# Moving two groups of VectorE work from between a scan and its use to behind the step, in the S5 loop of a two-block kernel

## The reference

```python
z = rms_norm(h, pre_mix_norm) @ w_in
z_rw, z_nsa, z_s5 = split(z)
o_rw  = rwkv7_mixer(token_shift(z_rw), ...)
o_nsa = nsa_mixer(z_nsa, ...)     # per query: compressed keys, selected keys, window keys
o_s5  = s5_mixer(z_s5, ...)       # y = C * linear_scan(lambda, B u), then a gated output
mix = concat([o_rw, o_nsa, o_s5]) @ w_out

# compressed branch of nsa_mixer, 15 compressed positions, 6 query heads
k_cmp = gelu(blocks(kc) @ w1_k) @ w2_k
v_cmp = gelu(blocks(vc) @ w1_v) @ w2_v
p_c = masked_softmax(q @ k_cmp.T * scale - slopes * distance)
o_c = p_c @ v_cmp
```

## Time and profile before

| what | value |
|---|---|
| median of 3 runs | 1343.27 us |
| the 3 runs | 1342.36, 1343.27, 1344.06 us |
| the profiled execution's own time | 1342.36 us |
| its span, first to last instruction | 1340.4 us |
| TensorE busy with matmuls | 1278.5 us (95%) |
| VectorE busy | 564.4 us (42%) |
| ScalarE busy | 621.8 us (46%) |
| GpSimd busy | 849.0 us (63%) |
| mean granted TensorE clock | 0.974 of full speed |

### The profile page before, as it was taken

The page is one execution under the profiler, slowest core; times in us unless marked ns, Lnnn a source line. Parts: engine busy times, 40 slices in busy tenths (PEclk is TensorE's granted clock), DMA queues, the critical chain, the costliest instruction groups (busy, mean ns, idle before and its releaser), DMA issues.

```text
span 1340.4 us, 25785 instructions
## 1 busy us (share of the span) xinstructions
PE 1278.5 (95%) x10737; PEld 1192.8 (89%) x10737; DVE 564.4 (42%) x1275; ACT 621.8 (46%) x962; POOL 849.0 (63%) x441
## 2 busy tenths in 40 slices
PE   7998989889999999899999999999999998999998
PEld 6984548679999999899999999999998888999998
DVE  5658686633666653513333203132222224433301
ACT  5531443136655644653544434554534454544442
POOL 7985400027798696564887786856745665788772
PEclk9998999989999999898999999999999999999999
DMA  8749995504455555334555554453648793455550
GB/s 266 205 158 371 345 334 206 189 1 158 145 177 183 173 174 188 126 122 162 165 182 189 173 174 157 145 165 98 191 127 263 233 291 123 139 181 188 174 173 32
DMA packets 232817, 242.82 MB, mean 181 GB/s; under 512 B 9068, under 2 KB 201726, under 8 KB 232702
## 3 DMA queue, kind: packets, MB, share of 16 engines
q1 hardware_dynamic: 232382, 241.08, 55.3%
q10 hardware_dynamic: 320, 0.10, 0.0%
HBM read 240.11 MB, written 1.05 MB: 180 GB/s over the span
## 4 chain that ended last, share of the span: by engine, by line
PE 83%; DVE 4%; ACT 2%; issue 1%; DVEq 0%; ACTq 0%
PE banks L548 81%; PE banks L1332 1%; DVE arena L1693 1%; DVE arena L1686 1%; ACT arena L2432 1%; DVE banks L1686 0%; DVE banks L1693 0%; ACT ring_hi L2432 0%; DVE arena L1699 0%; ACT hn_hi L2432 0%; PE banks L558 0%; PE banks L861 0%; PE banks L984 0%; ACT L2432 0%; DVE arena L1690 0%
## 5 line engine op out<-in xcount | busy, mean ns | idle before, releaser
L1613 POOL TENSOR_TENSOR ring_lo<-ring,ring_hi 128x2048 fp32r<-128x2048 f32 (+1 forms) x176 | 719.0, 4096 | 423.5 <-ACT ring_hi L2432 423.4
L548 PE MATMUL banks<-hn_hi,ring_lo 128*128 128x256 f32 (+1 forms) x1864 | 525.4, 287 | 0.0
L548 PE MATMUL banks<-hn_hi,ring_hi 128*128 128x256 f32 x1696 | 484.0, 289 | 11.8 <-ACT hn_hi L2432 11.0
L548 PE MATMUL banks<-hn_lo,ring_hi 128*128 128x256 f32 x1696 | 445.8, 283 | 0.0
L2432 ACT ACTIVATE ring_hi<-ring 128x2048 fp32r<-128x2048 f32 (+1 forms) x176 | 299.6, 1704 | 171.2 <-PE banks L548 127.3
L548 PEld LDWEIGHTS banks<-hn_hi,ring_lo 128*128 128x128 f32 (+1 forms) x1864 | 363.6, 196 | 0.1
L548 PEld LDWEIGHTS banks<-hn_hi,ring_hi 128*128 128x128 f32 x1696 | 333.1, 196 | 15.2 <-issue 9.4
L548 PEld LDWEIGHTS banks<-hn_lo,ring_hi 128*128 128x128 f32 x1696 | 310.5, 192 | 0.1
L2432 ACT ACTIVATE arena<-banks 128x256 f32<-128x256 f32 (+6 forms) x238 | 92.4, 409 | 242.7 <-PE banks L548 173.0
L548 PEld LDWEIGHTS banks<-arena 64*128 64x128 f32 (+4 forms) x1282 | 115.4, 178 | 62.2 <-issue 38.9
L548 PE MATMUL banks<-arena 128*64 128x128 f32 (+9 forms) x1282 | 143.1, 305 | 21.2 <-DVE arena L1686 8.7
(11 more groups left out here) (263 smaller groups left out, 1579.5 us busy)
## 6 DMA issues: line engine op xcount, KB each, us to landing
ring<-in_ada_w_dram SPq DMA_DIRECT2D x48, 1024.0 KB, 8.9
ring<-in_ffn_w_up_dram SPq DMA_DIRECT2D x44, 1024.0 KB, 5.2
ring<-in_w_up_dram SPq DMA_DIRECT2D x22, 1024.0 KB, 5.1
ring<-in_ffn_w_down_dram SPq DMA_DIRECT2D x16, 1024.0 KB, 4.9
ring<-in_w_kv_dram SPq DMA_DIRECT2D x15, 1024.0 KB, 5.5
ring<-in_w_in_dram SPq DMA_DIRECT2D x9, 1024.0 KB, 8.4
ring<-in_w_kv_dram SPq DMA_DIRECT2D x18, 512.0 KB, 4.0
ring<-in_attn_w_q_dram SPq DMA_DIRECT2D x18, 512.0 KB, 3.9
```

What stands on the lines that cost most here:

```text
L548: return nc.tensor.matmul(o, l, r, start=start, stop=stop, **k)
L1613: led.emit(g.tensor_tensor(low, raw, high.bitcast(F32), ALU.subtract), sem("lo_ready"))
```

## The change

`s5_scan` loses its argument `between`, so that the products follow the scans at once in every step. The body of `score_parts` moves to the start of the work of step 3 that follows `s5_y(1)`, and the body of `turned_probs` to the start of that of step 5, after `s5_y(3)` and ahead of the copies of ("cpv", s). No instruction is added or removed.

```diff
-            def s5_scan(j, between=None):
+            def s5_scan(j):
                 w = s5w[:, j % 2]
                 dve.wait_ge(sem("s5_in"), j + 1)
                 for x in range(2):
                     led.emit(v.tensor_tensor_scan(w[:, 3, x, :], z(2)[:, j:j + 1].broadcast_to([P, T]), w[:, 2, x, :],
                                                   0.0, MUL, ADD))
-                if between is not None:
-                    between()
                 settle()
                 tt(w[:, 0], w[:, 3], tabC[:, j, :].unsqueeze(1).broadcast_to([P, 2, T]), MUL)
                 tt(w[:, 1], w[:, 3], tabS[:, j, :].unsqueeze(1).broadcast_to([P, 2, T]), MUL, sem("s5_out"))
...
-            def score_parts():
-                b = take(("vc",))
-                for x in range(3):
-                    ts(vbd[0:96, :, x, :], shaped(b[0:96, 0:P], 2, HD), block3[0:96, x:x + 1], MUL,
-                       signal=freed(("vc",))[0] if x == 2 else None, value=freed(("vc",))[1] if x == 2 else None)
-                for s in range(2):
-                    for x in range(2):
-                        b = take(("cs", s, x))
-                        tt(csc[:, s, x::2, 0:NCMP], shaped(b[:, 0:96], 3, 32)[:, :, 0:NCMP], cbias[:, s, x::2, :], ADD,
-                           *freed(("cs", s, x)))
-
-            def turned_probs():
-                for s in range(2):
-                    b = take(("ct", s))
-                    copy(cpt[s][0:96, :, :], shaped(b[0:96, 0:T], 2, P), *freed(("ct", s)))
-
             s5_in(0)
             for j in range(8):
                 if j < 7:
                     s5_in(j + 1)
-                s5_scan(j, {3: score_parts, 5: turned_probs}.get(j))
+                s5_scan(j)
                 if j > 1:
                     s5_y(j - 2)
                 if j == 3:
+                    b = take(("vc",))
+                    for x in range(3):
+                        ts(vbd[0:96, :, x, :], shaped(b[0:96, 0:P], 2, HD), block3[0:96, x:x + 1], MUL,
+                           signal=freed(("vc",))[0] if x == 2 else None, value=freed(("vc",))[1] if x == 2 else None)
+                    for s in range(2):
+                        for x in range(2):
+                            b = take(("cs", s, x))
+                            tt(csc[:, s, x::2, 0:NCMP], shaped(b[:, 0:96], 3, 32)[:, :, 0:NCMP], cbias[:, s, x::2, :], ADD,
+                               *freed(("cs", s, x)))
                     settle()
...
                 elif j > 4:
                     if j == 5:
+                        for s in range(2):
+                            b = take(("ct", s))
+                            copy(cpt[s][0:96, :, :], shaped(b[0:96, 0:T], 2, P), *freed(("ct", s)))
                         for s in range(2):
                             b = take(("cpv", s))
                             copy(otok[:, s, :], b[:, 0:384], *freed(("cpv", s)))
```

## The result

The changed kernel took 1352.24 us (median of 4 runs, 1351.49 to 1353.58) against 1343.66 us (4 runs, 1342.36 to 1345.34): a ratio of 1.0064, 95% interval 1.0049 to 1.0079. It is slower by 8.6 us, where 2.4 were forecast and 1347.3 us was the upper end of the range. A later set with 12 runs of the changed kernel among 35 of the kernel before gave 1.0033 (1.0017 to 1.005), means of 1352.0 and 1346.8 us. The second figure is the better one: the 35 runs of the kernel before in that set spread from 1341.6 to 1351.1 us, and the first four all came from the lower half. All 33 runs of the changed kernel that are on record (21 with the first result, one of them the recorded one of 1351.78 us, and 12 later) lie between 1347.8 and 1354.0 us, 30 of them above 1350; their mean is 1352.2 us. One run of the kernel before took 1416 us, over 4% more than any other, and is left out of every mean here.

The account below looks back on a forecast made before the run. TensorE was taken to bound the kernel, at 83% of the chain, so VectorE counts only where TensorE waits. The terms 0.2 + 2.2 + 0 (clock) = +2.4 us on 1343.27 gave 1345.7 us, range 1344.2 to 1347.3.

Parts of the forecast that it names:

- The resume: TensorE restarting after VectorE's copies in step 5: 2.4 us later, 2.2 from step 5's order and 0.2 from step 3.
- What step 3 hands on: VectorE's reduction after step 3 starts 0.23 us later, so its step 5 scans do too; counted as 0.2 us.
- Step 3 covered: nsa_scores(0) on TensorE comes 2.2 us later, but the wait for step 5's copies hides it: adds 0.
- The clock: TensorE's low clock around the step 5 wait covers the same work as before: counted as 0.
- The rival of a longer low clock: Low clock after TensorE's longer idle time also covers more matmuls: +3.1 us in all, up to +3.6; chance 0.25.
- 116.57 for the end of the products: Step 3 time in the faster rival (chance 0.04): GpSimd's L1588 would start at 116.7 instead of 117.66, 1 us earlier.
- The base: Starting time of the forecast: 1343.27 us, the median of three runs, 0.91 us above the profiled 1342.36 us.

Follow-up runs that it names:

- e12: Changed kernel with the two copies of the turned probabilities on ScalarE instead of VectorE, step 3 kept in the changed order: 1344.6 us, 0.9981 of the kernel before.
- e7: Changed kernel with 12 unneeded matmuls added in TensorE's wait for the step 5 copies: 1348.0 us, 1.0008 of the kernel before.
- e13: Kernel before with 7 unneeded matmuls added at the head of nsa_scores(5), a plain delay of 1.7 us: 1348.7 us, ratio 1.0025.
- e14: Kernel before with 14 unneeded matmuls added at the head of nsa_scores(5), a plain delay of 3.3 us: 1349.8 us, ratio 1.0027.
- e2: Kernel before with only the copies of the turned probabilities moved behind the output of step 5: 1349.2 us, 1.0022 of the kernel before.

## Why the prediction was wrong

- **The resume (right).** "TensorE resumes ... at 132.77, against 130.36. This is 2.4 us later": 2.3 us in both traces of the changed kernel and 2.3 in step 5 only. The idle time ahead of it was 2.8 and 3.0 us, at the low end of the "3 to 5 us", and "every row of TensorE up to 166 us 2.4 us later" was 3.2 us in the first trace at head 6 and 2.3 in the second (52.50 against 50.17). The wait for the copies was on the path, as read from the program behind a piece that the chain calls "issue".
- **What step 3 hands on (too high by 0.2 us).** The products did slow to 1.63 us beside GpSimd's sums, as the Trainium skill (SBUF — State Buffer, "Who interferes with whom") has it. But GpSimd's next pair was also done sooner, 116.68 - 111.79 = 4.89 us behind the scans against 5.91, and the shift of the scores, 0.69 us long beside its L1589 before, took 0.41 without it. nsa_bias(0) starts 117.97 - 111.79 = 6.18 us behind the scans, 6.21 before. So 0.0 is handed on. The rows of before, and GpSimd's after:

```profile
118.66 0.69 DVE L1686 TENSOR_TENSOR arena<-arena 128x90 f32<-128x90 f32 x2
118.35 0.73 POOL L1589 TENSOR_TENSOR arena<-arena 128x256 f32<-128x256 f32 x1
```

```profile
115.96 0.72 POOL L1589 TENSOR_TENSOR arena<-arena 128x256 f32<-128x256 f32 x1
```

- **Step 3 covered (right).** +0.7 us (0.9988 to 1.0029) for step 3 alone, and no shift at the resume. e12 shows that it needs no cover from the copies: the late nsa_scores(0) only fills idle time, since VectorE is the next to be waited for.
- **The clock (the step that failed).** "The sum. 0.2 + 2.2 + 0 (clock)". The term was set to the same cost as before, and its bounds to -1.7 and +1.2 us, by looking only as far as the matmuls behind the resume. There the bounds held: 0.9 us up to head 6 in the first trace and 0.0 in the second. What was put at nothing, without a reason, is the clock behind that. In its place the runs give +2.6 us in the mean (5.2 less the 2.6 that remain with the wait filled) and +2.8 by the line through the single runs. The tail was 1184.5 and 1184.8 us in the two traces of the changed kernel; the kernel before's own four traces show that up to 8.5 us of it (1176.9 to 1185.4) come and go without any edit. The rival of a longer low clock, +0.7 to +1.2 us, had the right sign and less than half of the size. The one sum that does not come out of its rows, 116.57 for the end of the products (113.17 + 3.44 = 116.61 by the earlier trace rows), carries nothing.
- **The base.** The forecast took 1343.27 us and said that runs differ by 1.7 us. That was three runs; 35 runs in one set differ by 9.5 us and have a mean of 1346.8. The remaining 3.4 us between 8.6 and 5.2 are this.
- **Not settled:** why 30 of the 33 runs of the changed kernel are above 1350 us. The wait in step 5 is part of it (e7), a plain shift another (e13, e14), and step 5 only has quick runs that the whole change has not (e2). What in the rows of 170 to 210 us makes the clock fall in some runs of the kernel before and in nearly all of the changed kernel is open.

## What to carry to other kernels

A copy that the bound engine waits for belongs ahead of work that only a later step needs, however well the products fit behind the scans. Where TensorE's clock is low around that wait, its length alone is too low a price: here 2.3 us at the wait cost 5.2 us in the mean. Filled with work that was needed elsewhere the wait only moved; filled with idle matmuls it gave back 4.0 us in the changed kernel, and in the kernel before nothing that is clear of its uncertainty. Where every run has its clock on record, set its span against its time at the low level before a difference is put down to the edit. And a forecast within some tenths of a per cent needs the spread of the base from many runs, not from three.

## What was not expected of the hardware

One unchanged kernel took 1341 to 1354 us in 47 runs on one chip. Its low-clock time between 100 and 320 us was 27.3 us in a trace from that chip, and 37.6 and 54.6 us in two traces from another, with the same idle time of 1.14 us ahead of the same 14 records, 2.79 us long in the first two and 4.88 us in the last. Over 127 runs each microsecond at the low level went with 0.29 us of span. Adding 2.84 us of useless matmuls made a kernel 4.0 us faster.
